# Attention scores from float32 operands, and from stacked high and low halves

## The reference, cut to what matters

```
def attend(qb):                                             # kind A: 8 query heads, 2 key heads
    s = jnp.einsum('bqkgd,bskd->bkgqs', qb, k).astype(jnp.float32) * scale
    p = jax.nn.softmax(s, axis=-1).astype(v.dtype)
    return jnp.einsum('bkgqs,bskd->bqkgd', p, v)
...                                                         # kind B: 8 query and 8 key heads
s_win = jnp.einsum('bchd,bicjhd->bhcij', q_row, k_win).astype(jnp.float32) * scale
s_win = s_win + bias[None].astype(jnp.float32)
s_meta = jnp.einsum('bchd,bmhd->bhcm', q_row, km).astype(jnp.float32) * scale
```

## Time and profile before

| | us |
|---|---|
| median of 3 runs | 1212.04 (1210.35 to 1213.66) |
| the profiled execution | 1213.4 |
| its span, first to last instruction | 1211.6 |
| PE busy | 1157.0 (95%) |
| DVE busy | 841.1 (69%) |
| ACT busy | 602.8 (50%) |
| POOL busy | 263.1 (22%) |
| steps of the first layer's attention | about 78 to 212 |
| steps of the second layer's attention | about 319 to 438 |

### The profile page before, as it was taken

How to read it: one execution, slowest core, us unless ns; L and a number is a source line. 1 busy time by engine, 2 the same in 40 slices (tenths; PEclk the granted TensorE clock), 3 DMA queues, 4 the chain that set the end, 5 groups by cost and what they waited for, 6 DMA issues and landing times.

```text
span 1211.6 us, 23199 instructions
## 1 busy us (share of the span) xinstructions
PE 1157.0 (95%) x9292; PEld 1126.0 (93%) x9292; DVE 841.1 (69%) x1823; ACT 602.8 (50%) x940; POOL 263.1 (22%) x199
## 2 busy tenths in 40 slices
PE   6999999899999999999999989999999999999995
PEld 6989999899899998899999988888899999999995
DVE  6954444879444468787766789677855887777666
ACT  6454545453555546544444533565454564444453
POOL 1055543000655600000000058800372000000000
PEclk9999999999999999999999999999999999999998
DMA  6752343356523624555455533325454555554551
GB/s 239 181 193 106 105 126 85 140 175 166 182 105 109 168 73 174 192 201 183 168 178 180 207 140 105 140 71 168 159 134 150 177 182 194 188 176 166 191 199 35
DMA packets 47979, 188.07 MB, mean 155 GB/s; under 512 B 20856, under 2 KB 24184, under 8 KB 29312
## 3 DMA queue, kind: packets, MB, share of 16 engines
q1 hardware_dynamic: 47872, 186.58, 46.2%
HBM read 185.50 MB, written 1.06 MB: 154 GB/s over the span
## 4 chain that ended last, share of the span: by engine, by line
PE 76%; DVE 15%; ACT 4%; issue 2%; DMA 2%; POOL 0%; SPq 0%; DVEq 0%; ACTq 0%
PE line L1946 48%; PE result L1946 17%; DVE w_lo L1227 4%; PE turn L2072 1%; PE result L2106 1%; PE stat L2106 1%; PE score L2049 1%; ACT w_hi L798 1%; PE score L2053 1%; DMA raw<-in_weights 1%; DMA rel<-in_rpb 1%; PE score L2238 1%; DVE prod L1792 1%; DVE prod L1503 0%; DVE root L1249 0%
## 5 line engine op out<-in xcount | busy, mean ns | idle before, releaser
L781 POOL TENSOR_TENSOR w_lo<-raw,w_hi 128x512 fp32r<-128x512 f32 x184 | 258.9, 1439 | 592.0 <-ACT w_hi L798 591.9
L798 ACT ACTIVATE w_hi<-raw 128x2048 fp32r<-128x2048 f32 (+2 forms) x178 | 321.8, 1809 | 113.9 <-PE line L1946 42.3
L1946 PE MATMUL line<-x_hi,w_hi 128*128 128x256 f32 (+1 forms) x1144 | 339.1, 296 | 17.6 <-DVE x_lo L1270 8.6
L1227 DVE TENSOR_TENSOR w_lo<-raw,w_hi 128x512 fp32r<-128x512 f32 (+2 forms) x528 | 324.8, 660 | 5.5 <-ACT w_hi L798 3.0
L1946 PE MATMUL line<-x_hi,w_lo 128*128 128x256 f32 (+1 forms) x1144 | 327.1, 286 | 0.0
L1946 PE MATMUL line<-x_lo,w_hi 128*128 128x256 f32 (+1 forms) x1144 | 326.6, 285 | 0.0
L1946 PEld LDWEIGHTS line<-x_hi,w_hi 128*128 128x128 f32 x1144 | 218.5, 191 | 24.5 <-issue 16.5
L1946 PEld LDWEIGHTS line<-x_lo,w_hi 128*128 128x128 f32 x1144 | 217.9, 191 | 1.6
L1946 PEld LDWEIGHTS line<-x_hi,w_lo 128*128 128x128 f32 x1144 | 218.4, 191 | 0.0
L1946 PE MATMUL line<-y_hi,w_hi 128*128 128x256 f32 (+1 forms) x688 | 205.5, 299 | 3.6 <-DVE y_lo L1278 1.7
L1946 PE MATMUL line<-y_hi,w_lo 128*128 128x256 f32 (+1 forms) x688 | 196.0, 285 | 0.0
(11 more groups left out here) (323 smaller groups left out, 2107.1 us busy)
## 6 DMA issues: line engine op xcount, KB each, us to landing
raw<-in_weights SPq DMA_DIRECT2D x145, 1024.0 KB, 4.9
raw<-in_weights SPq DMA_DIRECT2D x32, 704.0 KB, 4.0
rel<-in_rpb SPq DMA_DIRECT2D x64, 64.0 KB, 6.4
h<-in_tokens SPq DMA_DIRECT2D x2, 544.0 KB, 6.1
raw<-in_weights SPq DMA_DIRECT2D x2, 512.0 KB, 5.7
rbias<-bias_by_distance SPq DMA_DIRECT2D x8, 128.0 KB, 5.5
out<-wide SPq DMA_DIRECT2D x4, 256.0 KB, 2.2
consts<-in_consts SPq DMA_DIRECT2D x1, 832.0 KB, 6.7
```

The lines of the kernel that those rows point to most:

```text
L781: pool.tensor_tensor(w_lo[:, u % CUT, at], raw[:, u % RAW, at], w_hi[:, u % CUT, at].bitcast(F32), ALU.subtract).then_inc(lo_pool, 1)
L798: act.activation(w_hi[:, v % CUT, first:n], raw[:, v % RAW, first:n], ACT.Copy).then_inc(hi_cut, 1)
L1227: dve.tensor_tensor(w_lo[:, u % CUT, at], raw[:, u % RAW, at], w_hi[:, u % CUT, at].bitcast(F32), ALU.subtract).then_inc(lo_cut, 1)
L1946: ins = pe.matmul(bank[:, 0:n], stay, move[:, first + k, 0:n], start=(k, m) == (0, 0), stop=(k, m) == (depth - 1, 2))
```

## The change

The score matmuls of the 64 four-part jobs no longer take float32 operands. For each pair of heads and each layer (a "unit" of four jobs, eight per layer) two fp32r operands are built:

- `q_stack`: for each half the 64 rows of that head's queries are rounded into the head's own 64 rows, and the low part is written into the other 64 rows.
- `k_stack`: for each half the head's keys, rounded, are written into both halves of the rows, and the keys' low part likewise.

A job's score is then two fp32r matmuls over all 128 rows that accumulate: `q_stack` by the keys' high parts, `q_stack` by the keys' low parts.

ACT writes the high parts (`stack_high`), DVE the low ones (`stack_low`), both by `halves_of`, in up to four parts for a unit: 0 and 1 are the queries of the two halves (one instruction of 64x256 on each engine), 2 and 3 the keys (two instructions of 64x272 on each engine). Kind A has only one set of keys in a layer, so that units 1 to 3 have parts 0 and 1 alone. Unit 0 is built whole among the head lines: by ACT at `at == 10`, by DVE at `at == 11`, after the line qb3 and its pieces and ahead of line vb0. Each further unit is built during the four first steps of the unit ahead of it, one part in a step (`stack_steps`): by ACT after the filler and before `turned_of`, by DVE at the end of the step. PE waits for the last part of a unit in `scores`. `ka_half` and the double width of `kb` go, with their memsets, and DVE writes a key line in two instructions instead of three.

```
+def units_of_heads(i):
+    return [(kind, c, (5 * i + (c + 1 if kind == "B" else 0)) % 2, JOBS[i].index((kind, c, 0, 0)))
+            for kind in "AB" for c in range(PAIRS)]
+def stack_steps(i):
+    at = {}
+    first = [u[3] for u in units_of_heads(i)] + [len(JOBS[i])]
+    for u in range(1, 2 * PAIRS):
+        for part in range(4):
+            at.setdefault(first[u - 1] + part, []).append((u, part))
+    return at
...
+    def halves_of(i, unit, part):
+        kind, c, place, _ = units_of_heads(i)[unit]
+        own, other = half_rows(part % 2), half_rows(1 - part % 2)
+        if part < 2:
+            src = (qa if kind == "A" else qb)[own, c, 0:SEQ]
+            to = q_stack[:, unit % 2, part]
+            return src, [to[own]], [to[other]], to[own]
+        if kind == "A" and c:
+            return None
+        half = part - 2
+        keys = ka[own] if kind == "A" else kb[own, c]
+        src = keys[:, META:META + TOK] if half == 0 else keys[:, 0:TOK]
+        hi, lo_ = k_stack[:, place, half, 0], k_stack[:, place, half, 1]
+        return src, [hi[own], hi[other]], [lo_[own], lo_[other]], hi[own]
...
-        pool.memset(ka_half[:, :], 0.0).then_inc(set_up, 1)
-        pool.memset(kb[:, :, :], 0.0).then_inc(set_up, 1)
...
+            def stack_high(unit, part):
+                if (i, unit, part) not in STACKED:
+                    return
+                if part == 0 and (i or unit >= 2):
+                    j, u = (i, unit - 2) if unit >= 2 else (i - 1, 2 * PAIRS + unit - 2)
+                    kind, c = units_of_heads(j)[u][:2]
+                    act.wait_ge(score_done, SCORE[(f"layer{j}", kind, c, 1, TILES - 1)] + 1)
+                src, high, _, _ = halves_of(i, unit, part)
+                for to in high:
+                    ins = act.activation(to, src, ACT.Copy)
+                ins.then_inc(stack_hi, 1)
+            for at, key in enumerate(HEAD_LINES):
+                head_step(at, key)
+                if at == 10:
+                    act.wait_ge(roped, 9 * i + (3 if W == TOK else 2))
+                    for part in range(4):
+                        stack_high(0, part)
...
+                for unit, part in stack_steps(i).get(t, []):
+                    stack_high(unit, part)
                 if 1 <= t <= J:
                     turned_of(jobs[t - 1], JOB[i] + t - 1)
...
-                    low_, high_ = half_rows(0), half_rows(1)
-                    dve.tensor_tensor(kb[low_, c, 0:TOK], bank[low_, 0:TOK], scale[low_, 0:TOK], ALU.mult)
-                    dve.tensor_tensor(kb[high_, c, TOK:TOK + META], bank[high_, SEQ:TOK], scale[high_, SEQ:TOK],
-                                      ALU.mult)
-                    dve.tensor_tensor(kb[high_, c, TOK + META:2 * TOK], bank[high_, 0:SEQ], scale[high_, 0:SEQ],
+                    dve.tensor_tensor(kb[:, c, 0:META], bank[:, SEQ:TOK], scale[:, SEQ:TOK], ALU.mult)
+                    dve.tensor_tensor(kb[:, c, META:META + TOK], bank[:, 0:TOK], scale[:, 0:TOK],
                                       ALU.mult).then_inc(kq_ready, 1)
...
+            def stack_low(unit, part):
+                if (i, unit, part) not in STACKED:
+                    return
+                src, _, low_, high = halves_of(i, unit, part)
+                dve.wait_ge(stack_hi, STACKED[(i, unit, part)])
+                for to in low_:
+                    ins = dve.tensor_tensor(to, src, high.bitcast(F32), ALU.subtract)
+                ins.then_inc(stack_ready, 1)
+            for at, (kind, c) in enumerate(HEAD_LINES):
+                head_step(at, kind, c)
+                if at == 11:
+                    for part in range(4):
+                        stack_low(0, part)
...
                 if t >= TAIL + 2:
                     rest_of_y(jobs[t - TAIL - 2])
+                for unit, part in stack_steps(i).get(t, []):
+                    stack_low(unit, part)
...
-                    ins = pe.matmul(s[:, 0:TOK], qa[:, c, t * P:(t + 1) * P], ka_half[:, half * TOK:(half + 1) * TOK],
-                                    start=True, stop=True)
...
-                    ins = pe.matmul(s[:, 0:TOK], qb[:, c, t * P:(t + 1) * P], kb[:, c, half * TOK:(half + 1) * TOK],
-                                    start=True, stop=True)
+                    kind, c, half, t = job
+                    unit = c + PAIRS * (kind == "B")
+                    pe.wait_ge(stack_ready, STACKED[(i, unit)])
+                    for low_ in range(2):
+                        ins = pe.matmul(s[:, 0:TOK], q_stack[:, unit % 2, half, t * P:(t + 1) * P],
+                                        k_stack[:, units_of_heads(i)[unit][2], half, low_], start=low_ == 0,
+                                        stop=low_ == 1)
```

More of the change, by code:

```diff
@@ L603, in hybrid_blocks_kernel @@
                    od_ready=od_ready, pp_ready=pp_ready, pg_raw=pg_raw)
+    def halves_of(i, unit, part):
[12 more added lines that the diff above has]
+        return src, [hi[own], hi[other]], [lo_[own], lo_[other]], hi[own]
+    STACKED, _n = {}, 0
+    for _i in range(DEPTH):
+        for _u in range(2 * PAIRS):
+            for _part in range(4):
+                if _part < 2 or _u == 0 or _u >= PAIRS:
+                    _n += 1
+                    STACKED[(_i, _u, _part)] = _n
+            STACKED[(_i, _u)] = _n
     row_dram = nc.dram_tensor("bias_by_distance", (SH, 2 * SEQ), F32).ap()
@@ L611, in hybrid_blocks_kernel @@
     qa = a1.sb("qa", [PAIRS, TOK])
-    ka = a1.sb("ka", [TOK])
+    ka = a1.sb("ka", [TOK + META])
     q_meta = a1.sb("q_meta", [PAIRS * META])
     qb = a1.sb("qb", [PAIRS, TOK])
-    ka_half = a1.sb("ka_half", [2 * TOK])
-    kb = a1.sb("kb", [PAIRS, 2 * TOK])
+    kb = a1.sb("kb", [PAIRS, TOK + META])
+    q_stack = a1.sb("q_stack", [2, 2, SEQ], F32R)
+    k_stack = a1.sb("k_stack", [2, 2, 2, TOK], F32R)
     head_out = a1.sb("head_out", [2, P])
@@ L874, in head_square @@
                     act.wait_ge(stat_done, STAT[(name, "head", n - 2)] + 1)
-                src = ka[:, :] if n == 0 else qa[:, n - 1]
+                src = ka[:, META:META + TOK] if n == 0 else qa[:, n - 1]
                 w = W if n else TOK
@@ L891, in layer, with head_step @@
             head_square(0)
-            for at, key in enumerate(HEAD_LINES):
+            def head_step(at, key):
                 cut_to(UNIT[(name, *key)] + CUT - 1)
@@ L904, in layer @@
                     v_by_token(key[1])
+            def stack_high(unit, part):
[15 more added lines that the diff above has]
+                        stack_high(0, part)
+            act.wait_ge(roped, 9 * i + (9 if W == TOK else 5))
+            act.wait_ge(kq_ready, 8 * i + 8)
             v_by_token(PAIRS)
@@ L1293, in layer @@
             if i == 0:
-                dve.wait_ge(set_up, 9)
+                dve.wait_ge(set_up, 7)
             rstd_of((name, "norm"), TOK, scale[:, :])
             def head_raw(n):
-                key, dst = ((name, "qa", n - 1), qa[:, n - 1, 0:W]) if n else ((name, "ka"), ka[:, :])
+                key, dst = ((name, "qa", n - 1), qa[:, n - 1, 0:W]) if n else ((name, "ka"), ka[:, META:META + TOK])
                 scaled_line(key, dst).then_inc(raw_head, 1)
@@ L1308, in rope @@
                 w = W if n else TOK
-                dst = ka[:, :] if n == 0 else qa[:, n - 1, 0:w]
+                dst = ka[:, META:META + TOK] if n == 0 else qa[:, n - 1, 0:w]
                 g = operand(f"k_gain{i}") if n == 0 else q_gain[:, i:i + 1]
@@ L1340, in layer, with head_step @@
             lo_after(name, "va")
-            for at, (kind, c) in enumerate(HEAD_LINES):
+            def head_step(at, kind, c):
                 if kind == "qa":
@@ L2006, in rot @@
             def rot(n):
-                src = ka[:, :] if n == 0 else qa[:, n - 1, 0:W]
+                src = ka[:, META:META + TOK] if n == 0 else qa[:, n - 1, 0:W]
                 bank = result_open((name, "rot", n))
```

18 lines of the change are left out of this document (6 added, 12 removed).

## The result

The changed kernel takes 1267.55 us (median of 4 runs, 1262.63 to 1268.6) where the kernel before, on the same chip, takes 1212.15: a ratio of 1.045, with a 95% interval of 1.0419 to 1.0481. It is slower by 55 us. The forecast was 1249 with a range of 1222 to 1266, so that the sign was right and the size too small: the time lies 1.6 us above the range. The profiled execution takes 1268.6 us, its span is 1266.8, that of before 1211.6: the difference to explain is 55.2 us.

What follows compares the result with a forecast made beforehand. PE was taken to set the pace, busy for 95% of the span. Savings, ACT copies, seven waits, head lines and clock summed as -9.7 + 1.0 + 25.6 + 10.0 + 10.4 = +37.3 us, giving 1249 us, range 1222 to 1266.

Steps and rivals of the forecast that it cites:

- the price of the clock: After six of seven score waits and both head waits, PE runs at 1.2 GHz: 8 x 1.3 = 10.4 us.
- 64 jobs: Score jobs on PE save 0.203 us each, at most 13.0 us; 9.7 us without blank steps and tight pair starts.
- `turn` behind ACT: In three blank steps of the first layer an ACT copy precedes the one PE awaits: 1.0 us.
- The price of the pair of matmuls: Two fp32r score matmuls of 272 columns take 0.252 us against 0.454 for the float32 score, saving 0.203 us a job.
- The seven places: Scores starting units 5, 6, 7 (first layer) and 4 to 7 (second) wait for DVE's last part: 25.6 us.
- The example's score: Step 24 of the second layer, starting unit 6: PE's score starts at 415.8 instead of 411.70, 4.1 us later.
- The head lines: Unit 0's six DVE subtractions delay line vb0 and PE's turn: about 5.2 and 4.8 us, together 10.0 us.
- waits that pile up: Rival, 13%: DVE late in every step, PE waits in more than seven steps, 14 to 20 us more, 1265 us.
- The stacks in time: Rival, 4%: DVE's low parts are done before PE reaches the score; savings of 9.7 to 11.4 us stand, 1201 to 1203.
- The clock that holds: Rival, 18%: the waits are as forecast but TensorE keeps 2.4 GHz, 1239 us.
- The pair that costs as much as a float32 score: Rival, 5%: the two fp32r matmuls cost what the float32 score did, no saving, 1259 us.
- Short waits without a lock: Rival, 17%: DVE and POOL don't block each other; about 2 us at each of seven places and each head, 1223 us.

Runs made afterwards that it cites:

- the kernel with only this part: Kernel before, each float32 score replaced by two fp32r matmuls on ready tiles of x, no stacks or added waits: 1200.18 us, ratio 0.9894.
- with POOL's writes: Changed kernel, POOL writing zeros by memset in place of its w_lo subtraction, so reading nothing in SBUF: 1225.76 us, ratio 1.0111.
- the kernel with the seven short waits: Kernel before, float32 scores, no stacks, PE waiting at the seven pair starts for the end of DVE's step: 1218.43 us, ratio 1.0041.
- the version with steps 0, 0, 0 and 2: Changed kernel, reordered head, ACT copies behind `turned_of`, DVE subtractions a step later after the maximum, parts in steps 0, 0, 0, 2: 1208.82 us, ratio 0.9943.
- the version before it: Changed kernel, parts in steps 0, 0, 1, 2, reordered head, ACT copies behind `turned_of`, DVE subtractions a step later: 1211.1 us, ratio 0.9992.
- the last versions: Changed kernel with parts, head, ACT copies and DVE subtractions all moved: 1211.1 us; first-key copies a step earlier 1208.82; also unit 0 spread over head lines 1211.4.
- the run with added matmuls: Changed kernel with 32 useless fp32r matmuls on PE ahead of each of the seven long waits: 1253.38 us, ratio 1.033.
- the control pair: POOL's w_lo subtraction replaced by a memset to zero, in the changed kernel: 1225.76 us, ratio 1.0111; in the kernel before: 1204.23 us, ratio 0.9941.

## Why the prediction was right and wrong

The step that failed is the price of the clock. The sum as the trace of after gives it has the waits as measured and the saving at its full 64 jobs, which was not measured in after itself (the forecast's lost savings are added back to the waits that they went into). The cost of the clock is what the distances between the starts of matmuls at the lower clock have over the same distances at the full clock:

| term | forecast, us | from the runs, us |
|---|---|---|
| 64 jobs | -13.0 | -13.0 |
| seven first scores of a pair | 25.6 + 1.4 = 27.0 | 29.0 |
| head lines | 10.0 | 9.1 |
| `turn` behind ACT | 1.0 + 1.8 = 2.8 | 7.9 - 1.8 = 6.1 |
| the clock | 10.4 | 21.6 |
| sum | 37.2 | 52.8 |

2.4 of the 55.2 us are left without a name.

- *The price of the pair of matmuls* was right. In after, around the score of step 22 of the second layer, whose two matmuls are merged in one row:

```profile
450.29 0.28 PE L2199 MATMUL result<-consts,head_out 128*128 128x128 f32 x1
450.32 0.50 PE L2133 MATMUL score<-k_stack,q_stack 128*128 128x272 f32 x2
450.66 0.28 PE L2027 MATMUL line<-y_hi,w_hi 128*128 128x256 f32 x1
```

  Here the first matmul of the pair starts 0.03 us behind a short one, and the second only 0.21 us after it. Behind another matmul of 272 columns, starts are 90.301, 90.428 and, of the line's matmul behind the pair, 90.553, 0.126 us each:

```profile
90.30 0.41 PE L2133 MATMUL score<-k_stack,q_stack 128*128 128x272 f32 x2
90.55 0.29 PE L2027 MATMUL line<-x_hi,w_hi 128*128 128x272 f32 x1
```

  And the kernel with only this part took 14.9 us off the span.

- *The seven places* were right by place and in the sum, 29.0 against 27.0 us, each place within 1 us of its forecast (they waited 3.1 to 4.5 us). The example's score was forecast 4.1 us late and waited for 4.45. Its chain had the forecast order, `w_hi`, tanh, copies, then subtractions beside POOL, but two of its links were off and partly made up for each other, which is luck. Counted from step 22's score (407.51 before, 450.32 after), part 3's copies start 5.8 us later instead of 5.1, since DVE was late before part 2 came, its `rel` held up beside POOL in step 21. And from the end of the copies the two subtractions need 1.9 us instead of 2.4, since only one meets a piece. The lock's share was right there: with POOL's writes this score waits for 2.91 us, 1.5 less.

```profile
448.09 1.68 DVE L1440 TENSOR_TENSOR rel<-rel,consts 128x512 f32<-128x512 f32 x1
```

- *The head lines* were right: 9.1 us against 10.0. In after DVE's six subtractions start at 66.14 and line vb0 is read at 72.74, forecast "at about 73.3"; PE's turn starts at 73.24:

```profile
66.14 2.82 DVE L1448 TENSOR_TENSOR q_stack<-qa,q_stack 64x256 fp32r<-64x256 f32 x2
68.98 3.73 DVE L1448 TENSOR_TENSOR k_stack<-ka,k_stack 64x272 fp32r<-64x272 f32 x4
72.74 0.44 DVE L1357 TENSOR_TENSOR prod<-line,scale 128x272 f32<-128x272 f32 x1
...
65.40 6.09 POOL L828 TENSOR_TENSOR w_lo<-raw,w_hi 128x512 fp32r<-128x512 f32 x4 [63.41 <-ACT w_hi L845]
...
73.24 0.90 PE L2081 MATMUL turn<-consts,prod 128*128 128x128 f32 x3 [4.93 <-DVE prod L1357]
```

  Four subtractions fall beside POOL's four pieces and take 1.4 us each, two behind them 0.44.

- *The clock is the term that failed*: 8 x 1.3 = 10.4 us, measured 21.6 (28.4 in after less 6.8 in before). The 1.3 us was read from one fall after a wait of 1.74 us, where the lower clock lasted 3.4 us. After the nine long waits (3.4 to 5.2 us from start to start) it lasted 6.8 us seven times, at 1.6 to 2.7 us each, and 3.4 us twice, at 1.2 to 1.5: 18.0 us together. Further 2.6 us come from two places where before had no fall (85.2 and 160.3), less 1.4 us of a fall that before alone had. And 2.1 us come from two waits that stand in both kernels. The first of them, 3.00 us long in both, in windows of before and then of after:

```profile
490.00:493.50 3.50, 3.05 (x10) 0.52 0.00 0
493.50:497.00 3.50, 3.50 (x32) 0.99 0.00 0
```

```profile
542.60:546.00 3.40, 2.20 (x6) 0.50 0.10 41
546.00:549.50 3.50, 3.50 (x19) 0.51 0.00 0
549.50:553.00 3.50, 3.50 (x32) 1.00 0.21 49
```

  The same wait, and the lower clock lasts twice as long. So 1.3 us was the price of the shorter of two stretches: nine waits at 1.3 to 2.7 us give 12 to 24 us, and the upper end of that alone would have put 14 us on the forecast. The old trace could not have given that end. Its five falls ahead of the end all lasted 3.4 us, also those at waits of 3.00 (490.45) and 3.26 us (711.29); the doubled stretch shows only in the later runs, also at that wait of 3.00 us in the kernel with the seven short waits. Nor is it the length of the wait alone: in the version with steps 0, 0, 0 and 2 the first score of the second layer waits for 1.6 us and the stretch is 6.8 us (317.2 to 324.0), and a `turn` that waits for 2.0 us is followed by a fall there (361.5) and by none in the version before it. What sets the length of a stretch at a given wait stays open here.

- *`turn` behind ACT's copies* was sized too small by 3.3 us. The 0.32 us of a copy was counted in three blank steps; the exponential that DVE's late maximum pushes back was left out of the sum and put with the rival of waits that pile up. The three longest of these waits lie outside the three counted steps: 1.9 us at 159.9 (0.2 before), and in the second layer 1.2 us at 364.8 (0.2 before) and 1.4 us at 393.0 (none before). Ahead of the last, DVE's maximum comes at 389.29, 2.15 us after its score instead of 1.0, behind `silu_b`, which took 1.01 us beside POOL, and a subtraction; the exponential, the `w_hi` and `turned` follow it.

- *The rivals.* The stacks in time was refuted as the change stands, but is nearly what the last versions reach by other placing. The clock that holds was refuted: it fell at each of the nine long waits, and without these falls at the seven places (the run with added matmuls) the span is 16.5 us shorter. The pair that costs as much as a float32 score was refuted. The waits that pile up gave 1265 us, and the result is nearest to that, but by another mechanism: of its 14 to 20 us of further waits, 3.3 us came, and the clock gave 11.2 more. That its number fits is luck. Short waits without a lock were refuted by the control pair; but in that kernel, with the lock gone, the seven waits were still 3.1 us each, so that the rival's 2 us was too small as well.

## What to carry to other kernels

An operand prepared by two in-order engines costs by where it stands in their lists rather than by its busy time: the same instructions, moved behind the work that others wait for and one step away from the engine that they wait on, took some 56 us off this kernel. Give each long new wait, beside its own length, a price for the clock whose upper end is twice the fall that the old trace happens to show. And look, before placing a two-input SBUF instruction on DVE, at what POOL reads in the same microseconds.

## What the hardware showed beyond what was expected

- A DVE subtraction of 64x256 or 64x272 takes 0.42 to 0.44 us alone. Beside subtractions of POOL, in the head lines, four in a row take 1.4 us each: DVE and POOL take turns, and POOL's pieces of 128x512 start 1.4 us apart there (67.21, 68.63, 70.04). Readers of PSUM keep their 0.42 to 0.45 us. Beside a memset of POOL nothing is slowed (0.418 to 0.440 us).
- The lower clock lasted 3.4 us or 6.8 us after a wait, also where the wait was the same. One such stretch mostly cost 1.2 to 1.5 us or 1.6 to 2.7 us.
- The seven waits of 0.7 us on average and at most 1.0 us for the end of DVE's step brought no fall of the clock.
